# Centring v instead of y: a mean product and a subtraction leave an RWKV-7 group loop

## What is computed

```
def step(state, inp):                       # state: value index i, key index j
    r_t, w_t, k_t, v_t, a_t, b_t = inp
    sa = einsum('bhij,bhj->bhi', state, a_t)
    state = state * w_t + sa[..., None] * b_t[:, :, None, :] + v_t[..., None] * k_t[:, :, None, :]
    return state, einsum('bhij,bhj->bhi', state, r_t)
y = scan(step)
mean = mean(y, axis=-1)                     # over the 64 value indices of a head
var  = mean(square(y - mean), axis=-1)
y = (y - mean) * rsqrt(var + 64e-5) * ln_w + ln_b
out = (y + bonus * v) * g
```

## Time and profile before

| what | value |
|---|---|
| median of 3 runs | 2751.24 us |
| the three runs | 2750.96, 2751.24, 2754.89 us |
| the profiled execution | 2754.32 us, its span 2752.6 us |
| TensorE busy | 2715.1 us, 99% of the span |
| VectorE, ScalarE, GpSimd busy | 45%, 30%, 5% |
| granted TensorE clock, mean | 0.997 |

### The profile page before, as it was taken

One profiled execution on the slowest core, in us unless ns is written; L12 is line 12 of the kernel. 1 busy time (PEld: TensorE's weight loads), 2 busy tenths in 40 slices (PEclk: granted clock), 3 DMA queues, 4 the chain that ended last, 5 costly groups with the idle time before them and its releaser, 6 DMA issues.

```text
span 2752.6 us, 44358 instructions
## 1 busy us (share of the span) xinstructions
PE 2715.1 (99%) x18368; PEld 2159.3 (78%) x18368; DVE 1238.5 (45%) x1916; ACT 816.0 (30%) x1340; POOL 133.6 (5%) x237
## 2 busy tenths in 40 slices
PE   9999999999999999998999999999999999999997
PEld 7877777777777766786888888888888888888886
DVE  6266666666435545344433333333333333324334
ACT  5222222222125444344432222322222222122233
POOL 4000111001121100000000000000000000000000
PEclk9999999999999999999999999999999999999999
DMA  4311111111235521221223222222223222222232
GB/s 167 120 55 49 48 48 51 45 48 49 62 102 204 180 70 61 85 92 62 91 93 100 98 94 99 96 94 99 94 96 99 93 98 99 92 98 93 98 100 100
DMA packets 72403, 249.33 MB, mean 91 GB/s; under 512 B 8960, under 2 KB 9088, under 8 KB 71104
## 3 DMA queue, kind: packets, MB, share of 16 engines
q1 hardware_dynamic: 65232, 222.62, 24.6%
q0 software_dynamic: 7024, 24.56, 2.7%
HBM read 236.93 MB, written 10.22 MB: 90 GB/s over the span
## 4 chain that ended last, share of the span: by engine, by line
PE 97%; DVE 1%; ACT 1%; issue 0%; DMA 0%; DVEq 0%; ACTq 0%; SPq 0%
PE ps L1176 28%; PE ps L1178 26%; PE ps L1177 26%; PE ps L1194 9%; PE ps L1407 1%; PE ps L1386 1%; PE ps L1395 1%; PE ps L1188 1%; PE ps L1246 0%; PE ps L1243 0%; PE ps L1226 0%; PE ps L1237 0%; DVE w_lo L725 0%; PE ps L1252 0%; PE ps L1221 0%
## 5 line engine op out<-in xcount | busy, mean ns | idle before, releaser
L725 DVE TENSOR_TENSOR w_lo<-w_raw,w_hi 128x1024 fp32r<-128x1024 f32 (+2 forms) x440 | 505.9, 1150 | 1136.4 <-ACT w_hi L437 1136.3
L437 ACT ACTIVATE w_hi<-w_raw 128x1024 fp32r<-128x1024 f32 (+2 forms) x440 | 438.9, 998 | 1537.5 <-PE ps L1178 1537.1
L1176 PE MATMUL ps<-act_hi,w_hi 128*128 128x512 f32 x1792 | 730.5, 408 | 1.9 <-DVE w_lo L725 1.9
L1178 PE MATMUL ps<-act_hi,w_lo 128*128 128x512 f32 x1792 | 700.7, 391 | 0.0
L1177 PE MATMUL ps<-act_lo,w_hi 128*128 128x512 f32 x1792 | 700.1, 391 | 0.0
L1176 PE MATMUL ps<-w_hi,mid_hi 128*128 128x512 f32 x1088 | 425.1, 391 | 3.9 <-DVE w_lo L725 2.5
L1177 PE MATMUL ps<-w_lo,mid_hi 128*128 128x512 f32 x1088 | 424.0, 390 | 0.0
L1178 PE MATMUL ps<-w_hi,mid_lo 128*128 128x512 f32 x1088 | 423.9, 390 | 0.0
L1176 PEld LDWEIGHTS ps<-act_hi,w_hi 128*128 128x128 f32 x1792 | 336.5, 188 | 94.8 <-issue 12.1
L1178 PEld LDWEIGHTS ps<-act_hi,w_lo 128*128 128x128 f32 x1792 | 336.8, 188 | 72.3
L1177 PEld LDWEIGHTS ps<-act_lo,w_hi 128*128 128x128 f32 x1792 | 337.0, 188 | 69.2 <-issue 6.0
(11 more groups left out here) (283 smaller groups left out, 2409.0 us busy)
## 6 DMA issues: line engine op xcount, KB each, us to landing
w_raw<-in_w_rest SPq DMA_DIRECT2D x320, 512.0 KB, 3.3
w_raw<-in_w_pairs SPq DMA_DIRECT2D x112, 384.0 KB, 3.0
x_t<-in_x_turned SPq DMA_DIRECT2D x8, 512.0 KB, 8.4
qk<-scr_qkv POOLq DMA_DIRECT2D x16, 256.0 KB, 3.1
h<-in_x POOLq DMA_DIRECT2D x4, 1024.0 KB, 11.4
out<-h SPq DMA_DIRECT2D x4, 1024.0 KB, 3.9
scr_qkv<-pad POOLq DMA_DIRECT2D x15, 256.0 KB, 4.1
w_raw<-in_w_lora SPq DMA_DIRECT2D x8, 288.0 KB, 7.3
```

The lines of the kernel that those rows point to most:

```text
L437: return nc.scalar.activation(dst, src, ACT.Copy, scale=scale)
L725: V.tensor_tensor(dst, w_raw[:, slot, 0:dst.shape[-1]], high.bitcast(F32), ALU.subtract).then_inc(s["w_split"], 1)
L1176: mm(dst, a_hi, b_hi, start=start, stop=False)
L1178: return mm(dst, a_lo, b_hi, start=False, stop=stop)
```

## The change

A third constant, `cen2` = `eye2` - 1/64, takes the place of `eye2` where v is turned to token rows. `v_tok` then holds v centred over its value index, and the output of the recurrence arrives centred. The mean product with its waits and the subtraction are gone; ScalarE copies bank 7 straight to `y_cent`, and the wait for the previous store moves from VectorE at p = 2 to ScalarE at the start of the group. In the last two groups the variance product waits for the last evacuation of bank 3 itself.

```
-        yb, yc, ysq, gs = s2("y_raw", [P, SEQ]), s2("y_cent", [P, SEQ]), ...
+        spare, yc, ysq, gs = s2("spare", [P, SEQ]), s2("y_cent", [P, SEQ]), ...
+        cen2 = s2("cen2", [P, L])
                                                       # GpSimd, constants
+            step(nc.gpsimd.tensor_scalar(cen2[:, :], eye2[:, :], -1.0 / L, None, ALU.add))
                                                       # ScalarE
-                    act.wait_ge(s["yc_ready"], f + 1)
+                    act.wait_ge(s["y_ev"], f + 1)
                     nc.scalar.activation(ysq[:, :], yc[:, :], ACT.Square).then_inc(s["ysq_ready"], 1)
...
                 if fin:
                     act.wait_ge(s["y_mm"], f + 1)
-                    copy(yb[:, :], bank(7)).then_inc(s["y_ev"], 1)
+                    if f:
+                        act.wait_ge(s["y_stored"], 16 * f)
+                    copy(yc[:, :], bank(7)).then_inc(s["y_ev"], 1)
                                                       # VectorE
-                if p == 2 and fin:
-                    dve.wait_ge(s["mean_mm"], f + 1)
-                    if f:
-                        dve.wait_ge(s["y_stored"], 16 * f)
-                    V.tensor_tensor(yc[:, :], yb[:, :], bank(3), ALU.subtract).then_inc(s["yc_ready"], 1)
                                                       # TensorE
-            def to_tokens(b, src):
+            def to_tokens(b, src, turner=eye2):
                 for c in range(NC):
-                    last = both(ps[:, b, part(c)], src[:, part(c)], eye2, True, True)
+                    last = both(ps[:, b, part(c)], src[:, part(c)], turner, True, True)
                 return last
...
-                if p == 1 and fin:
-                    pe.wait_ge(s["y_ev"], f + 1)
-                    pe.wait_ge(s["xT_ev"], LV * min(q, PAIRS))
-                    mm(bank(3), mean2[:, :], yb[:, :], start=True, stop=True).then_inc(s["mean_mm"], 1)
                 if p == 3 and elem:
                     pe.wait_ge(s["shifted"], q + 1)
-                    if fin:
-                        pe.wait_ge(s["yc_ready"], f + 1)
-                    elif q:
+                    if q:
                         pe.wait_ge(s["xT_ev"], LV * q)
-                    to_tokens(3, vv).then_inc(s["vtok_mm"], 1)
+                    to_tokens(3, vv, cen2).then_inc(s["vtok_mm"], 1)
...
                 if p == 5 and fin:
                     pe.wait_ge(s["ysq_ready"], f + 1)
                     if elem:
                         pe.wait_ge(s["vtok_ev"], q + 1)
                         pe.wait_ge(s["za_ev"], q + 1)
+                    else:
+                        pe.wait_ge(s["xT_ev"], LV * PAIRS)
                     mm(bank(3), mean2[:, :], ysq[:, :], start=True, stop=True).then_inc(s["var_mm"], 1)
```

More of the change, by code:

```diff
@@ L105, in hybrid_layer @@
         inv, t_lev = s2("inv", [P, SEQ]), s2("t_level", [P, SEQ])
-        yb, yc, ysq, gs = s2("y_raw", [P, SEQ]), s2("y_cent", [P, SEQ]), s2("y_sq", [P, SEQ]), s2("gate", [P, SEQ])
+        spare, yc, ysq, gs = s2("spare", [P, SEQ]), s2("y_cent", [P, SEQ]), s2("y_sq", [P, SEQ]), s2("gate", [P, SEQ])
         two = lambda name: [s2(f"{name}{i}", [P, SEQ]) for i in range(2)]
@@ L167, in hybrid_layer @@
             t_mm t_ev x_mm x_ev xT_mm xT_ev
-            z_mm z_ev u_mm u_ev s_mm s_ev y_mm y_ev mean_mm yc_ready ysq_ready var_mm var_eps var_sqrt rstd_ready gate_mm gate_ev y_fin y_stored
+            z_mm z_ev u_mm u_ev s_mm s_ev y_mm y_ev ysq_ready var_mm var_eps var_sqrt rstd_ready gate_mm gate_ev y_fin y_stored
             qkv_stored v_in y_landed y_hi y_lo vt_mm vt_ev qk_in bias_in bias_ready sink_in
```

## The result

| what | before | after |
|---|---|---|
| median of 11 runs each | 2754.03 us | 2761.68 us |
| ratio, 95% interval | | 1.0031, 1.0022 to 1.0039 |
| the profiled execution | 2754.32 us | 2760.43 us |
| its span | 2752.6 us | 2758.4 us |

The kernel became slower by 0.31%, some 8 us, where 6.9 us of gain were forecast. One of the 11 runs of before, at 4457.83 us, was disturbed; it counts in the median and is left out of the ratio.

What follows compares the result with a forecast made beforehand. TensorE, busy for 99% of the span, was taken as the bound. Eight mean products gave 6.9 us, all else nothing: 2751.24 - 6.9 = 2744.3 us on the median, range 2741.5 to 2749.0 us.

Steps and rivals of the forecast that it cites:

- The mean product: TensorE in the group loop: eight products removed, seven at 0.86 us and one at 0.87, 6.9 us gained.
- What else changes, at nothing: Unchanged token-row products, the square's new wait, xT_ev waits and one added GpSimd instruction: no cost to the end.
- The subtraction: VectorE, 0.68 us eight times, 5.4 us in all; off TensorE's path, so nothing on the end.
- the moved store wait: ScalarE at a group's start waits for the previous store; 7.6 us of cover in the tightest case, cost nothing.
- the new constant: One GpSimd instruction of 64 columns ahead of the flag consts; hidden by 7.9 us, cost nothing.
- Rivals 2, 3 and 4: 2: product hid wait, no change (0.04); 3: whole busy time, 8.9 us (0.06); 4: ScalarE store stall, 2756.7 us (0.02).
- Rival 1: Gain given back at a_dec: six full groups keep only 0.31 us each; 3.6 us, 2747.6 us; chance 0.10.
- the tightest: VectorE's a_dec, done 0.31 us before its product; VectorE's work moves with TensorE, so the 0.31 us stay.
- From there to the end each stage hangs on TensorE as before.: After the a_dec margin, through the kernel's end: later stages follow TensorE, so the sum stays 6.9 us.

Runs made afterwards that it cites:

- after_head0: The changed kernel with the head of TensorE's MLP loop placed at slot 0 of a fetch block; 2745.79 us, ratio 0.9969 to the kernel before.
- before_head0: The kernel before the change with the head of TensorE's MLP loop placed at slot 0 of a fetch block; 2752.59 us, ratio 0.9997.
- after_head200: The changed kernel with the head of TensorE's MLP loop placed at slot 200 of a fetch block; 2746.19 us, ratio 0.9971 to the kernel before.
- after_head236: The changed kernel with the head of TensorE's MLP loop placed at slot 236 of a fetch block; 2752.11 us, ratio 0.9996 to the kernel before.
- after_warm15: The changed kernel with 15 instead of 12 idle matmuls at the start of TensorE's program; 2745.82 us, ratio 0.9973 to the kernel before.

## Why the prediction was wrong

**The mean product: right.** 0.86 us start to start was forecast for seven groups and 0.87 for the last. The copies of bank 7, which bound the first seven, show 5.87 us for them where the forecast has 6.02: 0.84 to 0.90 in six of them and 0.69 in the first. The busy time, 8.9 us, would have been too much.

**What else changes, at nothing: right, but for the 0.17 us of the first group.** The subtraction, the moved store wait, the new constant and the values of v show no other cost: no TensorE wait in the list from 200 to 780 us, and the copy of bank 7 is released by TensorE. Rivals 2, 3 and 4 did not come, and nothing ended on ScalarE's store. Rival 1 showed in one group of six, with 0.17 us (0.86 - 0.69).

**The margins: the tightest held in five groups of six.** `a_dec` was to stay some 0.31 us ahead of its product. In the second to the sixth fin group it ends 0.30 us ahead, as before. In the first it doesn't; timelines of VectorE and TensorE after:

```profile
301.01 0.28 DVE L971 SCALAR_TENSOR_TENSOR state<-ps,g_last,state_decayed 128x64 f32<-128x64 f32 x1 [0.43 <-issue]
...
303.87 0.69 DVE L862 SCALAR_TENSOR_TENSOR a_dec<-kk_norm,g_pad 128x512 f32<-128x512 f32 x1
```

```profile
304.34 0.33 PE L1193 MATMUL ps<-z_s,invT 64*64 64x64 f32 x4
304.62 1.15 PE L1193 MATMUL ps<-a_dec,k_dec 64*64 64x64 f32 x32
```

It ends at 304.56, 0.06 us ahead. TensorE's `z_s,invT` came 306.83 - 304.34 = 2.49 us earlier than before, `a_dec` only 306.68 - 304.56 = 2.12: VectorE's row of work has a gap of 0.43 us ahead of `state` that was not there before, and that nothing in the trace releases; its cause stays open. The product starts 0.28 us behind `z_s,invT`, where before it was 306.99 - 306.83 = 0.16 us; so some 0.12 us are probably a wait there, though the list of waits shows none. This is the group that is only 0.69 us shorter. So a margin below the gain can break, and this one has no room for another edit of this size.

**The step that failed:** "From there to the end each stage hangs on TensorE as before." The data do, the waits too; the instructions don't. The sum put the effect of the edit behind the group loop at nothing, and gave no reason for the program itself. But TensorE's program is fetched too, in the 115 or 160 packets, and where the MLP's loop starts in its block depends on the count of instructions ahead of it. Taking out 38 moved the head from place 30 to place 248 of 256, and its laps lost 16.1 us. Of these, five times 2.5 us are the stall itself (176.6 - 174.08), and in two laps 1.7 us more. This is what TensorE's clock did; timeline of TensorE after, behind the second stall:

```profile
1862.07 0.79 PE L1175 MATMUL ps<-act_hi,w_hi 128*128 128x512 f32 x1 [2.17 <-DVE h L1029]
1862.66 0.63 PE L1176 MATMUL ps<-act_lo,w_hi 128*128 128x512 f32 x1
1863.08 0.63 PE L1177 MATMUL ps<-act_hi,w_lo 128*128 128x512 f32 x1
```

The records take 0.63 us for 0.39, and the window from 1850 to 1870 us has a granted clock of 0.91 on the mean: for a while it was at 1.2 GHz after TensorE had stood for 2.2 us. The two laps with such a fall are those of 178.3 and 178.4 us.

**The balance.** Where the MLP's first `h` starts, after was 10.0 us ahead, 3.1 more than forecast. Before had two such clock falls ahead of the MLP (7.9 and 857.8 us), after none: the granted clock from 0 to 20 and from 850 to 870 us is 0.91 before and 1.00 after, in both windows. At 1.7 us each that is 3.4, and 6.9 + 3.4 = 10.3 us, near the 10.0. The first copy of bank 7 shows the one at 7.9 us: it ran 1.65 us earlier (275.85 - 274.20), before any product that the change took out. In after_head0 both falls were there again, and the lead was 7.0 us. So this surplus is one execution's luck, not a gain of the change. Then 10.0 - 16.1 = -6.1 us, as the `h` rows (-6.2) and the profiled executions (2754.32 - 2760.43) say.

**What could have been seen.** The page of before listed 115 instruction packets, and its DMA view none in five laps of a loop of 1598 instructions. That is 6.2 blocks' worth, so it touches 7 blocks or 8, as its head lies. I read neither row, since nothing there was busy. The Trainium skill would have pointed at it (Runtime: NRT & Kernel Launch, Instruction fetch mechanics): it gives TensorE's instruction memory as 128 KiB, filled in blocks of 16 KiB, and says that a taken branch to a place that isn't held forces a fetch. The trace agrees with the fetch at the branch. That page also lets a branch reach without a fetch only what lies in a window of two such blocks; here 7 blocks stayed through five laps without one packet, so for TensorE the measurement decides against it. And 128 KiB are 8 such blocks, yet a body over 8 did not stay without the hint: room has to be left for the one fetched ahead, if the inference above is right.

## What to carry to other kernels

An edit to one engine's program moves every later instruction of that engine; when a long loop follows, compare the instruction packets and the lap times before you credit or blame the edit, and give both versions the same place for the loop. A loop whose body touches 7 blocks or 8 as its head lies, such as this one of 1598 instructions, wants its head pinned at the start of a block: it is one option, it costs nothing that could be measured (before_head0, 0.9997), and it turned this change from 0.3% slower to 0.3% faster. A wait in the list that falls once a lap, at the same place behind the branch, and whose releaser makes no sense, is to be held against the instruction queue first.

## What the runs showed of the hardware

- TensorE kept a loop over 7 blocks of 256 instructions without a fetch (laps of 174.08 us, 115 or 116 packets in all) and fetched 9 packets in every lap when it touched 8 (160 or 161 in all), unless the branch had the hint. One of the 9 began ahead of the branch back, when the body had just entered its eighth block: in the first lap 1.1 us ahead in after_head200, 4.5 in after_head236, 6.7 in after.
- The fetch that matters is the second one behind the branch: it began at 1682.49 us, when the first had let the loop's head run, and its instructions ran at 1685.10, 2.6 us later. 56 instructions in the head's block hid it but for 0.3 us at most, 20 left 1.1 to 1.3 us of a lap, 10 to 4 left 1.9 to 2.7.
- The 2.2 us stall was followed by a fall of the granted clock to half in two laps of five in the profiled execution, and in three of five in that of after_warm13; the fall cost 1.7 us more.
- The waits' releaser for a fetch stall is a VectorE instruction in some kernels and "issue" in others: nothing in the row says that instructions were missing.
